# Dense products of a decoder step: split fp32r matmuls replaced by plain fp32 matmuls, with a ring of six weight buffers

## The reference, cut to what matters

```python
def swiglu(h, w_in, w_out):
    gu = h @ w_in
    return (jax.nn.silu(gu[..., :FFN_DIM]) * gu[..., FFN_DIM:]) @ w_out

# layer 0: ffn, gated DeltaNet, ffn; then the shared latent K/V; layer 1: ffn, MLA, ffn
x = x + 0.5 * rmsnorm(swiglu(rmsnorm(x, norm_pre[layer, 0]), ffn_in[layer, 0], ffn_out[layer, 0]), norm_post[layer, 0])
h = rmsnorm(x, norm_pre[layer, 1])
y, S_new, cv_new = gdn_mixer(h, ...)        # layer 0
y = mla_mixer(h, cos, sin, kc, kpe, ...)    # layer 1
x = x + rmsnorm(y, norm_post[layer, 1])
x = x + 0.5 * rmsnorm(swiglu(rmsnorm(x, norm_pre[layer, 2]), ffn_in[layer, 1], ffn_out[layer, 1]), norm_post[layer, 2])
```

## Time and profile before

| | |
|---|---|
| median of 3 runs | 1430.91 us (1429.84 to 1431.15) |
| span of the profiled execution | 1428.4 us |
| VectorE busy | 889.8 us (62%), 1480 instructions |
| ScalarE busy | 742.7 us (52%), 1218 instructions |
| POOL busy | 161.9 us (11%), 229 instructions |
| HBM read | 213.07 MB, 154 GB/s over the span with what is written |

### The profile page before, as it was taken

The page is one execution under the profiler, slowest core; times in us unless marked ns, Lnnn a source line. Parts: engine busy times, 40 slices in busy tenths (PEclk is TensorE's granted clock), DMA queues, the critical chain, the costliest instruction groups (busy, mean ns, idle before and its releaser), DMA issues.

```text
span 1428.4 us, 29450 instructions
## 1 busy us (share of the span) xinstructions
PE 1412.2 (99%) x11003; PEld 1346.2 (94%) x11003; DVE 889.8 (62%) x1480; ACT 742.7 (52%) x1218; POOL 161.9 (11%) x229
## 2 busy tenths in 40 slices
PE   9999999999999999999999999999999999999998
PEld 9999999999888999999999999999877699999998
DVE  6655535999888675554376555349755548655534
ACT  6555424788646565553265555346533346555423
POOL 0111000010110011110011111001144201111000
PEclk9999999999999999999999999999999999999999
DMA  6444443344242254444434444444599643444441
GB/s 242 163 149 151 153 154 136 119 152 146 100 155 98 89 177 147 147 147 148 147 119 166 154 151 147 154 147 150 187 293 285 212 156 118 169 152 150 147 147 67
DMA packets 50776, 221.01 MB, mean 155 GB/s; under 512 B 6705, under 2 KB 23474, under 8 KB 28802
## 3 DMA queue, kind: packets, MB, share of 16 engines
q1 hardware_dynamic: 38882, 189.07, 38.0%
q0 software_dynamic: 6192, 24.64, 5.2%
q10 hardware_dynamic: 5616, 6.16, 1.3%
HBM read 213.07 MB, written 6.77 MB: 154 GB/s over the span
## 4 chain that ended last, share of the span: by engine, by line
PE 94%; DVE 3%; ACT 2%; issue 1%; DMA 0%; DVEq 0%
PE psum L283 16%; PE psum L287 15%; PE psum L282 15%; PE psum L381 8%; PE psum L380 8%; PE psum L382 8%; PE psum L2681 2%; PE psum L2639 2%; PE psum L309 1%; PE psum L300 1%; PE psum L325 1%; PE psum L304 1%; PE psum L2510 1%; PE psum L311 1%; PE psum L315 1%; PE psum L1553 1%
## 5 line engine op out<-in xcount | busy, mean ns | idle before, releaser
L270 DVE TENSOR_TENSOR w_lo<-raw,w_hi 128x2048 fp32r<-128x2048 f32 x159 | 368.6, 2318 | 290.5 <-ACT w_hi L263 290.4
L263 ACT ACTIVATE w_hi<-raw 128x2048 fp32r<-128x2048 f32 x155 | 296.7, 1914 | 351.7 <-PE psum L382 207.8
L282 PE MATMUL psum<-h_hi,w_hi 128*128 128x320 f32 x1504 | 446.0, 310 | 0.0
L283 PE MATMUL psum<-h_lo,w_hi 128*128 128x320 f32 x1504 | 444.1, 309 | 0.0
L282 PEld LDWEIGHTS psum<-h_hi,w_hi 128*128 128x128 f32 x1504 | 282.1, 188 | 2.6 <-issue 1.3
L283 PEld LDWEIGHTS psum<-h_lo,w_hi 128*128 128x128 f32 x1504 | 283.4, 188 | 0.5
L287 PE MATMUL psum<-h_hi,w_lo 128*128 128x320 f32 x1504 | 251.3, 309 | 0.0
L287 PEld LDWEIGHTS psum<-h_hi,w_lo 128*128 128x128 f32 x1504 | 228.3, 188 | 0.3 <-DVE w_lo L270 0.3
L380 PE MATMUL psum<-hid_hi,w_hi 128*128 (+1 forms) x704 | 217.4, 309 | 0.0
L381 PE MATMUL psum<-hid_lo,w_hi 128*128 (+1 forms) x704 | 217.4, 309 | 0.0
L382 PE MATMUL psum<-hid_hi,w_lo 128*128 (+1 forms) x704 | 217.4, 309 | 0.0
(11 more groups left out here) (459 smaller groups left out, 1957.4 us busy)
## 6 DMA issues: line engine op xcount, KB each, us to landing
raw<-wts SPq DMA_DIRECT2D x161, 1024.0 KB, 4.8
h_plain<-cache_t POOLq DMA_DIRECT2D x44, 160.0 KB, 3.7
h_plain<-cache_t SPq DMA_DIRECT2D x44, 160.0 KB, 3.7
arena<-s POOLq DMA_DIRECT2D x4, 1024.0 KB, 7.2
sgs<-arena POOLq DMA_DIRECT2D x4, 1024.0 KB, 4.6
marena<-cache_t POOLq DMA_DIRECT2D x20, 160.0 KB, 4.0
marena<-cache_t SPq DMA_DIRECT2D x20, 160.0 KB, 3.6
raw<-cache_c SPq DMA_DIRECT2D x16, 128.0 KB, 4.2
```

The lines of the kernel that those rows point to most:

```text
L263: act.activation(w_hi[c0 % 2][:, :], raw_of(c0, pair)[:, :], ACT.Copy).then_inc(hi_ready, 1)
L270: eng.tensor_tensor(w_lo[c0 % 2][:, :], raw_of(c0, pair)[:, :], w_hi[c0 % 2][:, :].bitcast(F32), ALU.subtract).then_inc(lo_ready, 1)
L282: pe.matmul(outs[n], wtile(w_hi, c0, tile0 + n * K + k), src_hi(k), start=(k == 0), stop=False)
L283: pe.matmul(outs[n], wtile(w_hi, c0, tile0 + n * K + k), src_lo(k), start=False, stop=False)
```

## The change: what it does

Every dense product is one `pe.matmul` of plain fp32 operands. The high and low tensors, all splits and their semaphores go; the operand tensors are hx, hid, h2 and ol in fp32. The weight chunks land in six ring buffers, wring[0..5] (the room of raw, w_hi and w_lo), and TensorE reads them there. A chunk's load waits for chunk_done of the chunk six before. The attention's scratch moves from raw to the room of ol_lo, so the ring is free of it, and SP's queue carries the loads of six chunks (uv to the first of ffn3) between the page loads of attention. The rope key's weight is 64 columns wide instead of 128 (high and low side by side).

```diff
-        raw = [sb(f"raw{i}", [P, CHUNK]) for i in range(2)]
-        w_hi = [sb(f"w_hi{i}", [P, CHUNK], F32R) for i in range(2)]
-        w_lo = [sb(f"w_lo{i}", [P, CHUNK], F32R) for i in range(2)]
+        wring = [sb(f"wring{i}", [P, CHUNK]) for i in range(NSLOT_W)]
...
+        def load_chunk(sp, c):
+            if c >= NSLOT_W:
+                sp.wait_ge(chunk_done, c - NSLOT_W + 1)
+            sp.dma_start(slot_of(c)[:, :], io["wts"][c, :, :]).then_inc(w_landed[c % NSLOT_W], 16)
...
+        def weights_landed(pe, c):
+            pe.wait_ge(w_landed[c % NSLOT_W], 16 * (c // NSLOT_W + 1))
...
+        def dense_in(pe, c, N, K, outs, src, tile0=0):
+            weights_landed(pe, c)
             for n in range(N):
                 for k in range(K):
-                    pe.matmul(outs[n], wtile(w_hi, c0, tile0 + n * K + k), src_hi(k), start=(k == 0), stop=False)
-                    pe.matmul(outs[n], wtile(w_hi, c0, tile0 + n * K + k), src_lo(k), start=False, stop=False)
-                if n == 0:
-                    pe.wait_ge(lo_ready, c0 + 2 * pair + 1)
-                for k in range(K):
-                    last = pe.matmul(outs[n], wtile(w_lo, c0, tile0 + n * K + k), src_hi(k), start=False, stop=(k == K - 1))
+                    last = pe.matmul(outs[n], wtile(c, tile0 + n * K + k), src(k), start=(k == 0), stop=(k == K - 1))
             return last
...
+        def dense_pair(pe, c, outs0, outs1, first, stat_q):
+            weights_landed(pe, c)
+            for k in range(KT):
+                pe.wait_ge(h_ready, first + k + 1)
                 for n, o in enumerate(outs0):
+                    last = pe.matmul(o, wtile(c, n * KT + k), hx[:, k, :], start=(k == 0), stop=(k == KT - 1))
+                if k == KT - 1:
                     last.then_inc(chunk_done, 1)
+                if k == 0:
+                    weights_landed(pe, c + 1)
                 for n, o in enumerate(outs1):
+                    last = pe.matmul(o, wtile(c + 1, n * KT + k), hx[:, k, :], start=(k == 0), stop=(k == KT - 1))
             last.then_inc(chunk_done, 1)
+            pre_stat_pe(pe, stat_q)
...
-                for kk, (s_hi, s_lo) in enumerate(srcs):
-                    pe.matmul(o, wtile(w_hi, c0, 2 * m + kk), s_hi, start=(start and kk == 0), stop=False)
-                    pe.matmul(o, wtile(w_hi, c0, 2 * m + kk), s_lo, start=False, stop=False)
-                    last = pe.matmul(o, wtile(w_lo, c0, 2 * m + kk), s_hi, start=False, stop=(stop and kk == 1))
+                for kk, src in enumerate(srcs):
+                    last = pe.matmul(o, wtile(c, 2 * m + kk), src, start=(start and kk == 0), stop=(stop and kk == 1))
...
-            act.activation(w_hi[c0 % 2][:, :], raw_of(c0, pair)[:, :], ACT.Copy).then_inc(hi_ready, 1)
...
-            eng.tensor_tensor(w_lo[c0 % 2][:, :], raw_of(c0, pair)[:, :], w_hi[c0 % 2][:, :].bitcast(F32),
-                              ALU.subtract).then_inc(lo_ready, 1)
...
-                pe.matmul(bank[5][:, 0:TOK], kr_w[:, k, :], h2_hi[:, k, :], start=(k == 0), stop=False)
-                last = pe.matmul(bank[5][:, 0:TOK], kr_w[:, k, :], h2_lo[:, k, :], start=False, stop=(k == KT - 1))
+                last = pe.matmul(bank[5][0:ROPE, 0:TOK], kr[:, k, :], h2[:, k, :], start=(k == 0), stop=(k == KT - 1))
...
             for i in range(2, NUN):
                 load_pages(sp, 0, aland, i)
                 load_plain(sp, 0, spland, i - 2)
+                if i - 4 in range(BASE["mla_out"] + 5 - BASE["uv"]):
+                    load_chunk(sp, BASE["uv"] + i - 4)
...
+            for c in range(BASE["mla_out"] + 5, NCHUNK):
+                load_chunk(sp, c)
```

More of the change, by code:

```diff
@@ L36 @@
 CHUNK = 16 * P
+NSLOT_W = 6
 EPS = 1e-6
@@ L164, in build @@
         yflat = y[:, :, :].rearrange("p k t -> p (k t)")
+        AW = 27672
+        H2 = 2 * KT * TOK
         s1 = ExitStack()
[L169 to L174, removed]
+        hx = sb("hx", [P, KT, TOK], F32, s1)
+        sb("beside_h", [P, KT, TOK], F32, s1)
+        hid = sb("hid", [P, HT, TOK], F32, s1)
+        h2 = sb("h2", [P, KT, TOK], F32, s1)
         f_g = [sb(f"f_g{i}", [P, TOK], F32, s1) for i in range(2)]
@@ L235, in build @@
[L235 to L252, removed]
@@ L265, in split_lo @@
[L265 to L269, removed]
-            eng.tensor_tensor(w_lo[c0 % 2][:, :], raw_of(c0, pair)[:, :], w_hi[c0 % 2][:, :].bitcast(F32),
-                              ALU.subtract).then_inc(lo_ready, 1)
[L273 to L279, removed]
+        y_out = sem("y_out")
@@ L306, in dense_pair @@
[L306 to L317, removed]
@@ new lines, in first_pre_dve, with pre_act @@
+        def first_pre_dve(dve):
+            for m in range(KT):
+                if m == 0:
+                    dve.wait_ge(x_landed, 16)
+                elif m in (2, 4):
+                    dve.wait_ge(x_rest[m // 2 - 1], 16)
+                dve.tensor_tensor(y[:, m, :], x[:, m, :], x[:, m, :], ALU.mult).then_inc(x_squared, 1)
+            square_tree(dve, 0)
+        def pre_act(act, s, gain):
+            for m in (1, 2, 0, *range(3, KT)):
+                act.wait_ge(x_ready, KT * (s - 1) + ((3, 1, 2)[m] if m < 3 else m + 1))
+                if m > 0:
+                    act.activation(hx[:, m, :], x[:, m, :], ACT.Identity, scale=gain(m)).then_inc(h_ready, 1)
+                act.activation(y[:, m, :], x[:, m, :], ACT.Square).then_inc(x_squared, 1)
@@ L726, in down @@
-            def down(c0, k, pair=0, **kw):
-                srcs = [(hid_hi[:, bass.ds(k + q, 1), :].rearrange("p a t -> p (a t)"),
-                         hid_lo[:, bass.ds(k + q, 1), :].rearrange("p a t -> p (a t)")) for q in range(2)]
-                dense_out(pe, c0, pair, srcs, **kw)
-            c += HT
-            down(c, 0, start=True, stop=False, free=HT * (f + 1) - 1)
-            with pe.Fori(0, (HT // 2 - 3) // 2) as j:
-                for i in range(2):
-                    down(c + 1 + i, 2 * (1 + i) + 4 * j, pair=j, start=False, stop=False)
@@ L742, in ffn_act, with tile @@
+            c += HT
+            for j in range(HT // 2):
+                last = j == HT // 2 - 1
+                pe.wait_ge(hid_ready, HT * f + 2 * j + 2)
+                dense_out(pe, c + j, [hid[:, 2 * j + q, :] for q in range(2)], start=(j == 0), stop=last,
+                          done_sem=y_done if last else None, free=HT * (f + 1) - 1 if j == 0 else None)
         def ffn_act(act, f):
-            c = BASE[f"ffn{f}"]
-            def tile(i, c0, t, pair=0, j=0, root=None):
-                split_hi(act, c0 + 2, pair)
+            def tile(i, t, root=None):
@@ L799, in tile @@
                 dve.wait_ge(gu_ready, HT * f + t + 1)
-                dve.tensor_tensor(f_h[i][:, :], f_gu[i][:, :], f_e[i][:, :], ALU.mult).then_inc(hid_ready, 1)
-                dve.wait_ge(hid_hi_ready, HT * f + t + 1)
-                one = lambda a: a[:, bass.ds(t, 1), :].rearrange("p a t -> p (a t)")
-                dve.tensor_tensor(one(hid_lo), f_h[i][:, :], one(hid_hi).bitcast(F32), ALU.subtract) \
-                   .then_inc(hid_lo_ready, 1)
-            tile(0, c, 0, split_first=True)
@@ L829, in ffn_dve @@
-            if c + 2 + 2 * n < NCHUNK and 2 * n < HT // 2 - 1:
-                split_lo(dve, c + 2 + 2 * n)
         def ffn_pool(pool, f):
@@ L2074, in gout_pe @@
             c = BASE["gdn_out"]
-            pe.wait_ge(ol_ready, 2)
-            pe.wait_ge(hi_ready, c + 1)
-            pe.wait_ge(lo_ready, c + 1)
+            pe.wait_ge(oh_ready, 2)
+            weights_landed(pe, c)
             def bank_of(m):
-                o = bank[m][:, 0:TOK]
                 for k in range(2):
-                    pe.matmul(o, wtile(w_hi, c, 2 * m + k), h_hi[:, k, :], start=(k == 0), stop=False)
-                    pe.matmul(o, wtile(w_hi, c, 2 * m + k), h_lo[:, k, :], start=False, stop=False)
-                    last = pe.matmul(o, wtile(w_lo, c, 2 * m + k), h_hi[:, k, :], start=False, stop=False)
+                    last = pe.matmul(bank[m][:, 0:TOK], wtile(c, 2 * m + k), hx[:, k, :], start=(k == 0), stop=False)
                 return last
@@ L2321, in tiles @@
                     for k in range(4):
-                        pe.matmul(o[n], wtile(w_hi, c, 4 * n + k), q_hi(k), start=(k == 0), stop=False)
-                        pe.matmul(o[n], wtile(w_hi, c, 4 * n + k), q_lo(k), start=False, stop=False)
-                pe.wait_ge(lo_ready, c + 1)
-                for n in ns:
-                    for k in range(4):
-                        last = pe.matmul(o[n], wtile(w_lo, c, 4 * n + k), q_hi(k), start=False, stop=(k == 3))
-                return last
+                        last = pe.matmul(o[n], wtile(c, 4 * n + k), qn(k), start=(k == 0), stop=(k == 3))
+                return last
+            c = BASE["uq"]
+            weights_landed(pe, c)
+            for k in range(4):
+                pe.wait_ge(qn_ready, k + 1)
+                for n in range(4):
```

(16 more changed lines are left out.)

688 lines of the change are left out of this document (165 added, 523 removed).

## The result

| | before | after | ratio, 95% interval |
|---|---|---|---|
| median of 4 runs each, us | 1430.68 | 1689.48 (1687.49 to 1690.63) | 1.1809 (1.1792 to 1.1825) |
| span of the profiled execution, us | 1428.4 | 1685.8 | |
| VectorE / ScalarE busy, us | 889.8 / 742.7 | 439.2 / 404.9 | |

The change makes the kernel 18% slower. The forecast was 1691 us.

The account below looks back on a forecast made before the run. TensorE, busy 99%, was taken to bound the kernel. The 1428.4 us span plus 258.8 for dense records, -6 for waits and +8 for attention gave 1689.2, about 1691 us as run median; range 1668 to 1716 for 8 in 10.

Parts of the forecast that it names:

- The count and the pitch: Dense products on TensorE: 5264 plain fp32 records at 0.269 us replace 7888 fp32r records at 0.1467 us, +258.8 us.
- The weight loads hidden: Dense products: new fp32 weights can come at least every 0.12 us, so at 320 columns the moving columns set the pitch.
- The rest, 271.2 us: Span outside the dense records: GDN core, attention, statistics and the few waits, 271.2 us of 1428.4 before the change.
- waits that go: Late splits or semaphores at uv start, attention start, GDN core and kernel start: -6 us together, between 0 and -14.
- +8 for attention: Six 1 MB weight chunks among attention's page loads on SP's queue: +8 us, between 0 and +17.
- the lead of the plain pages: Attention: a plain load is there about 4 us before use, part of 4 to 8 us of lead absorbing chunk delay.
- Removal is worth nothing in the feed-forwards: Feed-forwards: the splits are completely covered by matmuls, so taking them away gains nothing there.
- One record a product: Rival at the dense products: a plain fp32 product costs 0.269 us, time about 980 us; chance 4%.
- loads not hidden: Rival at the dense products: part of the 190 ns weight load enters the pitch, likely 0.28, 1750 us; chance 5%.
- the splits paced 15 us or more beyond the waits: Rival: GDN core and MLA projections speed up by 15 us or more, time 1670 us; chance 4%.
- Attention harder bound by DMA: Rival in attention: chunks ahead of pages on SP's queue delay units, up to +30 us, 1713 us; chance 5%.
- One pass for reduced fp32: Dense products, estimate from the skill: 0.133 us per fp32r matmul, three 0.400, against 0.533 for plain fp32: +349 us.

Follow-up runs that it names:

- the half-column run: Changed kernel with dense_in and dense_out running 160 of 320 columns on every matmul not first of its sum: 1137.15 us, ratio 0.7949 to before.
- the trace with idle work: Changed kernel plus an unread ScalarE copy and VectorE subtraction in each of 88 feed-forward tiles: 1688.48 us, ratio 1.1813 to before.

## Why the prediction was right, step by step

**The count and the pitch: right.** 5264 dense records were forecast; L242's 3008, L302's 1408 and 224, and the small lines add up to just that. Their pitch is 0.2692 for the 0.269 read off the last eight matmuls of the kernel before: 5264 x 0.2692 = 1417 us against 1416.0. One short row of the right shape was enough, because its record count against the code's four calls was looked at too. Recorded durations alone would have misled: three times 309 ns is more than twice 432, so the change would have looked like a gain.

**The weight loads hidden: right.** Read from L2510, and shown by the half-column run: 0.135 us at 160 columns with a new weight for each product.

**The rest, 271.2 us: 1685.8 - 1417.1 = 268.7 after.** The forecast had -6 for waits that go and +8 for attention, +2 in all; it is -2.5.
- **Attention: +4.8, not +8.** This is what its units take more (114.64 for 109.80 us, the table above). The mechanism came as told: the lead of the plain pages is used up after some units and L2312 waits for cache_c. But only three units are further apart than before, 8.9, 9.6 and 8.5 us for 7.8, 7.1 and 7.2 (scores at 1253.56, 1262.45, 1272.06 and 1280.51), and not all from the sixth on. Two terms of the estimate were off, against each other. I took 314 GB/s as the rate for the pages; full engines move 373, and a unit's 2.10 MB in its 7.1 to 7.9 us is already 270 to 300 GB/s, so the old rate was what attention asked for and no limit. By 373 a unit with a chunk takes 3.15 MB / 373 GB/s = 8.4 us, about 1 us behind for each of six and not 2.1. With the lead of 4 to 8 us that I credited, 0 to 2 us would then have come through; 4.8 did, so the lead was put too large as well. The two errors pull opposite ways, so that the term was no further off is in part luck.
- **The waits that go: -7.4 by difference, -6 forecast, and mostly not where named.** The table takes each stage from its first record to the next stage's first (the last feed-forward to the end of the span), less its dense records times 0.1467 or 0.2692; attention's 16 units are left out.

| stage | before, us | after, us | difference | forecast |
|---|---|---|---|---|
| start to the first dense record | 7.39 | 6.00 | -1.4 | -1 |
| four feed-forwards | 25.93 | 22.01 | -3.9 | 0 |
| DeltaNet input projections | 8.84 | 7.96 | -0.9 | 0 |
| DeltaNet core and output | 94.43 | 93.73 | -0.7 | -2 |
| MLA down and up projections, latent | 7.00 | 7.58 | +0.6 | -2, with the row below |
| attention up to its first scores | 2.45 | 2.09 | -0.4 | in the row above |
| attention, last scores to uv | 11.67 | 11.00 | -0.7 | -1 |
| uv and output | 3.72 | 3.71 | 0 | 0 |

- **"Removal is worth nothing in the feed-forwards" failed.** Most of the 3.9 us lie in dense_pair, where the operand tiles arrive one by one. Before, its 96 records take 14.84 us from first to last start, 0.9 more than 95 pitches; after, its 64 take 17.03, 0.07 more than 63. That is 0.8 us in each of its four stages: 2.5 us in three feed-forwards, and nearly all of the 0.9 in the DeltaNet input projections. The wait of L309 on the high operand (1.2 us in four) is gone with it. Where the other 1.4 us of the feed-forwards went was not traced. The forecast kept the other wait of L309, on the first tile (it stayed, 1.8 for 1.7), and held that TensorE is never caught up after it. In the kernel before it was.
- **A new wait of 1.8 us in the MLA projections** (L2005 on the normed query) was in none of my steps. Before, the 16 low-weight matmuls of the latent projection (L2156, 2.75 us from 985.25) stood between the query's statistic and the first use of the normed query, and covered the way through ScalarE and VectorE. The plain version has no such matmuls. A split's third matmul is work, and here it was also cover.

**The rivals.** One record a product and loads not hidden are refuted by the pitch. That the splits paced 15 us or more beyond the waits is refuted by the stages: DeltaNet's core and the MLA projections together changed by 0.1 us. Attention harder bound by DMA was right in kind and too large by far.

**The skill's four passes.** The Trainium skill, FP8 and Floating Point Precision, section TensorE Precision Notes, with its four passes for true fp32 fits 2 x 0.2692 = 0.538 us a product, four times 320 columns at 2.4 GHz (0.533). One pass for reduced fp32, which I had worked out from that section, gave +349 us as an estimate; measured was +257 in the span. The fp32r records come at 0.1467 us and not at 0.1333, and that is about 106 us over the 7888 of them.

## What to carry to other kernels

Where TensorE is full, count the records a product leaves in the trace and multiply by the distance between starts, never by the recorded duration; the plain fp32 product (0.538 us at 320 columns) costs more than three split ones (0.440 in fp32r, 0.407 in 16 bits), and the work taken off other engines buys next to nothing back. Look for what a matmul that goes away had covered: the one new wait was of that kind. If the split scheme stays, 16-bit halves are the faster ones here. With TensorE faster still, the limit was the turn-taking of the two engines that split, so look at the order of their work and not only at its sum. Bulk loads that have slack belong outside a stage whose own loads nearly fill the DMA engines.

## What the runs showed of the hardware

- An fp32r record of 320 columns comes every 0.1467 us and one of 160 every 0.112; a 16-bit one of 320 every 0.1356; a plain fp32 one of 320 every 0.2692 and one of 160 about 0.135. So the fp32r stream has a price over its columns that plain fp32 and 16 bits don't show. The load (188 ns recorded against 98 in 16 bits) is a candidate, but plain fp32's load is recorded as 190 ns and fits under 0.135, and the two points of fp32r fit neither simple law. This stays open.
- fp16 and bf16 are alike to 0.2 us of 1359.
- POOL's 128x320 fp32 product takes 864 ns alone and 2778 ns where it overlaps VectorE's 128x2048 fp32 subtraction of 2.28 us (at 67.81 and 68.04 us in the trace with idle work): it ends 0.7 us after the subtraction. The subtraction takes 2281 ns in the mean.
- Waits of 1.0 and 2.0 us within 10 us, in a stage that otherwise keeps TensorE busy, were followed by a time at the lower of the two clocks, 1.2 GHz: the granted clock is 0.54 in 1271 to 1273 and 0.61 in 1273 to 1275, 0.91 in the mean of the 20 us, and 1.00 where the waits were taken away. But the trace with idle work has waits of 1.4, 1.2 and 2.4 us in the same stage and 1.00 throughout. So such waits can be followed by a dip and need not be.
